# A two-stage transformer kernel on one core: values in high and low parts, up projections with joined products, and three steps moved

## The reference, cut to what matters

```python
def retention_mixer(h_ctx, h_lat, w_in, decay_logit, norm_g, w_out, need_ctx):
    ...
    # per head (4 heads, key width 256, value width 512), for latents and context:
    att = jnp.einsum('bihd,bjhd->bhij', q, k) * decay_mask
    o = jnp.einsum('bhij,bjhv->bihv', att, v)          # "the values"
    ...
def retention_output(o, g, norm_g, w_out):
    ...
    on = ((of - mu) * lax.rsqrt(var + EPS)).astype(g.dtype).reshape(b, n, h * dv) * norm_g
    return (on * jax.nn.silu(g)) @ w_out

# second block, each of two layers:
x = _layer_norm(DEEPNORM_ALPHA * x + h, ln1_g[i], ln1_b[i])
mlp = jnp.einsum('bsf,fd->bsd', jnp.square(jax.nn.relu(jnp.einsum('bsd,df->bsf', x, w_up[i]))), w_down[i])
...
x = _layer_norm(DEEPNORM_ALPHA * x + mlp + ple, ln2_g[i], ln2_b[i])
```

## Time and profile before

| | |
|---|---|
| median of 3 runs | 2045.7 us (2042.88 to 2045.72) |
| the profiled execution | 2045.57 us, span from first to last instruction 2043.8 us |
| PE busy | 2002.7 us, 98% of the span |
| DVE busy | 1289.1 us, 63% |
| ACT busy | 848.2 us, 42% |
| granted clock of PE, mean | 0.995 |
| PE's full-precision values (line 2382) | 41.8 us busy |

### The profile page before, as it was taken

One profiled execution on the slowest core, in us unless ns is written; L12 is line 12 of the kernel. 1 busy time (PEld: TensorE's weight loads), 2 busy tenths in 40 slices (PEclk: granted clock), 3 DMA queues, 4 the chain that ended last, 5 costly groups with the idle time before them and its releaser, 6 DMA issues.

```text
span 2043.8 us, 27094 instructions
## 1 busy us (share of the span) xinstructions
PE 2002.7 (98%) x11112; PEld 1702.3 (83%) x11112; DVE 1289.1 (63%) x1588; ACT 848.2 (42%) x991; POOL 68.4 (3%) x121
## 2 busy tenths in 40 slices
PE   7999999999999999999999999999999999999998
PEld 5778787778888888877779998898899978989997
DVE  3877879556545354586775555766855567677555
ACT  4332323223322122446664443554544346545442
POOL 0000000000111000000000000000000000000000
PEclk9999999999999999999999999999999999999999
DMA  9543444333454343332137655545665554546552
GB/s 342 173 161 124 144 144 139 109 131 107 143 167 157 116 129 129 103 107 100 49 105 217 185 167 163 190 168 167 206 200 191 166 170 157 196 158 214 188 185 81
DMA packets 250734, 319.30 MB, mean 156 GB/s; under 512 B 10097, under 2 KB 166034, under 8 KB 250098
## 3 DMA queue, kind: packets, MB, share of 16 engines
q1 hardware_dynamic: 234880, 262.24, 40.2%
q0 software_dynamic: 14416, 53.14, 7.8%
q10 hardware_dynamic: 1314, 2.18, 0.3%
HBM read 316.47 MB, written 1.05 MB: 155 GB/s over the span
## 4 chain that ended last, share of the span: by engine, by line
PE 82%; DVE 8%; DVEq 4%; ACT 2%; SPq 1%; issue 1%; ACTq 1%; DMA 1%
PE ps L2305 13%; PE ps L2306 13%; PE ps L2300 6%; PE ps L2855 6%; PE ps L2319 5%; PE ps L2315 5%; PE ps L2316 5%; PE ps L2861 5%; PE ps L2865 5%; PE ps L2862 5%; PE ps L2248 4%; PE ps L2772 2%; PE ps L2775 2%; PE ps L2771 2%; DVE w_lo L1239 1%; DVE raw L1370 1%
## 5 line engine op out<-in xcount | busy, mean ns | idle before, releaser
L1239 DVE TENSOR_TENSOR w_lo<-raw,w_hi 128x2048 fp32r<-128x2048 f32 (+1 forms) x244 | 553.3, 2272 | 304.5 <-ACT w_hi L602 303.7
L602 ACT ACTIVATE w_hi<-raw 128x2048 fp32r<-128x2048 f32 (+1 forms) x244 | 461.7, 1897 | 267.3 <-PE ps L2300 157.4
L2305 PE MATMUL ps<-w_hi,big_hi 128*128 128x512 f32 x760 | 299.1, 393 | 0.9 <-DVE big_lo L1729 0.7
L2306 PE MATMUL ps<-w_hi,big_lo 128*128 128x512 f32 x760 | 296.6, 390 | 0.0
L2315 PE MATMUL ps<-hT_hi,w_hi 128*128 128x512 f32 (+1 forms) x512 | 192.5, 381 | 3.1 <-ACT arena L710 2.0
L2316 PE MATMUL ps<-hT_lo,w_hi 128*128 128x512 f32 (+1 forms) x512 | 190.4, 377 | 0.0
L2861 PE MATMUL ps<-h_hi,w_hi 128*128 128x256 f32 x768 | 189.7, 285 | 0.0
L2862 PE MATMUL ps<-h_lo,w_hi 128*128 128x256 f32 x768 | 188.3, 283 | 0.0
L2305 PE MATMUL ps<-w_hi,hT_hi 128*128 128x512 f32 x416 | 168.9, 406 | 4.8 <-DVE hT_lo L1244 4.8
L2305 PEld LDWEIGHTS ps<-w_hi,big_hi 128*128 128x128 f32 x760 | 142.8, 188 | 30.4 <-issue 1.0
L2306 PEld LDWEIGHTS ps<-w_hi,big_lo 128*128 128x128 f32 x760 | 143.0, 188 | 28.8 <-issue 0.5
(11 more groups left out here) (309 smaller groups left out, 3072.5 us busy)
## 6 DMA issues: line engine op xcount, KB each, us to landing
raw<-ffn_w_in SPq DMA_DIRECT2D x88, 512.0 KB, 5.1
raw<-w_in SPq DMA_DIRECT2D x80, 512.0 KB, 4.6
raw<-w_up SPq DMA_DIRECT2D x64, 512.0 KB, 4.7
raw<-w_down SPq DMA_DIRECT2D x64, 512.0 KB, 4.6
raw<-ret_w_in SPq DMA_DIRECT2D x48, 512.0 KB, 5.4
front<-ada_w POOLq DMA_DIRECT2D x24, 1024.0 KB, 5.5
raw<-ffn_w_out SPq DMA_DIRECT2D x40, 512.0 KB, 4.5
raw<-ada_w POOLq DMA_DIRECT2D x64, 256.0 KB, 4.1
```

What stands on the lines that cost most here:

```text
L602: act.activation(SPLIT_HI[PAIR_OF[u]][:, 0:m], raw[:, RAW_OF[u], 0:m], ACT.Copy).then_inc(sem["hi_ready"], 1)
L1239: op(SPLIT_LO[PAIR_OF[u]][:, 0:m], raw[:, RAW_OF[u], 0:m], SPLIT_HI[PAIR_OF[u]][:, 0:m].bitcast(F32), ALU.subtract).then_inc(sem["lo_ready ...
L2305: pe.matmul(out, x[0][:, t * P:(t + 1) * P], w, start=start, stop=False)
L2306: pe.matmul(out, x[1][:, t * P:(t + 1) * P], w, start=False, stop=False)
```

## The change

1. The values of retention heads 0 to 2 are computed as hi*hi, lo*hi and hi*lo. ScalarE writes PT_HI and VN_HI, VectorE PT_LO and VN_LO. VN_LO is written by `values_lo`, on VectorE's list behind the second `weigh()` of the next head; `values` waits for it. The scores are written to another place in the arena, PT_LO over them.
2. The up projection's high products have hi and lo part of x side by side as one moving operand of 512 columns, into two halves of a PSUM bank; a unit has two banks, two units alternate. ScalarE copies the lo half, VectorE adds the hi half, and one more operation does ReLU and square.
3. Rows 2 and 3 of the modulation are copied by VectorE, and both are transposed before head 0's strip goes on; VectorE splits the weights of qb0 between two halves of `rows_split`.
4. Head 0's unit g0 goes to the other banks and doesn't wait for qk_read; the unit g1 does.
5. In layer 1 `ln2_first` stands before `x_lo(0, 6)`, and `ln2_second` before the split of the third unit.

```diff
-        h2_hi = sb("h2_hi", [P, KD, 256], F32R, hT_at)
-        h2_lo = sb("h2_lo", [P, KD, 256], F32R, hT_at + 4 * 2048)
+        h2_both = sb("h2_both", [P, 2, KD, 256], F32R, hT_at)
+        h2_hi, h2_lo = (h2_both[:, j, :, :] for j in range(2))
...
+        def gate_banks(h):
+            return head_banks(h)[0 if h else 1]
...
+        VN_HI = sb("VN_HI", [P, 4, 512], F32R, arena_at + 4 * 4096)[:, :, :]
+        VN_LO = sb("VN_LO", [P, 4, 512], F32R, big_at + 4 * (8192 + 4096))[:, :, :]
+        PT_HI, PT_LO = (sb(name, [P, 6, 256], F32R, arena_at + 4 * a)[:, :, :] for name, a in (("PT_HI", 0), ("PT_LO", 2048)))
...
+        UP_PAIR = (6, 0)
...   ScalarE
             split(FIRST_END["qb0"])
-            front(3)
-            row(0, 8960, 2)
-            front(4)
-            row(1, 9472, 3)
             act.wait_ge(sem["mod_ready"], 4)
...
+                act.wait_ge(sem["sc_read"], h + 1)
+                if h < 3:
+                    act.activation(PT_HI, PT, ACT.Copy).then_inc(sem["pt_hi"], 1)
                 used(f"vb{h}")
-                act.activation(VN[:, :, :], ps[:, a:a + 4, :], ACT.Copy).then_inc(sem["v_read"], 1)
+                act.activation(VN_HI if h < 3 else VN, ps[:, a:a + 4, :], ACT.Copy).then_inc(sem["v_read"], 1)
...
-                    act.activation(HID[:, n % 4, :], bank(UP_BANK[n % 4]), ACT.Relu).then_inc(sem["up_read"], 1)
+                    act.activation(HID[:, n % 4, :].rearrange("p (j n) -> p j n", j=2), ps[:, UP_PAIR[n % 2]:UP_PAIR[n % 2] + 2, 256:512], ACT.Copy).then_inc(sem["up_low"], 1)
...   VectorE
             rows_split(1, 0)
-            split(FIRST_END["qb0"])
+            row(0, 8960, 3)
+            row(1, 9472, 4)
             mod_cols(2, 0, 1)
             mod_cols(3, 0, 3)
             rows_split(0, 4)
+            split(FIRST_END["qb0"])
             rows_split(1, 4)
...
+            def values_lo(h):
+                a = head_banks(h)[0]
+                dve.wait_ge(sem["v_read"], h + 1)
+                lo(VN_LO, ps[:, a:a + 4, :], VN_HI).then_inc(sem["v_lo"], 1)
...
                 weigh()
+                if h:
+                    values_lo(h - 1)
                 ahead(f"qa{h}")
...
                 weigh()
+                if h < 3:
+                    dve.wait_ge(sem["pt_hi"], h + 1)
+                    lo(PT_LO, PT, PT_HI)
                 ahead(f"vb{h}")
...
                 split(base + 1)
+                if l:
+                    ln2_first(base)
                 x_lo(0, 6)
                 split(base + 2)
                 if l == 0:
                     last_residual(1, 1)
                 else:
-                    ln2_first(base)
+                    ln2_second(base, l - 1)
                     split(base + 3)
-                    ln2_second(base, l - 1)
...
-                    dve.wait_ge(sem["up_read"], s.next("up_read"))
-                    op(HID[:, n % 4, :], HID[:, n % 4, :], HID[:, n % 4, :], ALU.mult).then_inc(sem["sq2_ready"], 1)
+                    dve.wait_ge(sem["up_low"], s.next("up_low"))
+                    h = HID[:, n % 4, :].rearrange("p (j n) -> p j n", j=2)
+                    op(h, h, ps[:, UP_PAIR[n % 2]:UP_PAIR[n % 2] + 2, 0:256], ALU.add).then_inc(sem["up_read"], 1)
+                    drain()
+                    stt(out=h, in0=h, scalar=0.0, in1=h, op0=ALU.max, op1=ALU.mult).then_inc(sem["sq2_ready"], 1)
...   TensorE
             to_cols(2, 8960)
+            to_cols(3, 9472)
             pe.wait_ge(sem["h_part"], 4)
             strip(4, "qa0", hT, 0, 4, (0, 1), True, False, (2, 3))
-            to_cols(3, 9472)
...
-                pe.wait_ge(sem["v_read"], h + 1)
-                pe.wait_ge(sem["sc_read"], h + 1)
+                if h < 3:
+                    pe.wait_ge(sem["v_lo"], h + 1)
+                else:
+                    pe.wait_ge(sem["v_read"], h + 1)
+                    pe.wait_ge(sem["sc_read"], h + 1)
...
+                        pe.matmul(bank(a + t), PT_HI[:, m, q], VN_HI[:, j, :], start=(n == 0), stop=False)
+                        pe.matmul(bank(a + t), PT_LO[:, m, q], VN_HI[:, j, :], start=False, stop=False)
+                        i = pe.matmul(bank(a + t), PT_HI[:, m, q], VN_LO[:, j, :], start=False, stop=(n == len(keys) - 1))
...
-                pe.wait_ge(sem["qk_read"], h + 1)
-                feature(a, f"g0{h}", 0, 0)
+                g = gate_banks(h)
+                if h:
+                    pe.wait_ge(sem["qk_read"], h + 1)
+                feature(g, f"g0{h}", 0, 0)
...
-                used(feature(a + 1, f"g0{h}", 1, 0))
+                used(feature(g + 1, f"g0{h}", 1, 0))
+                pe.wait_ge(sem["qk_read"], h + 1)
...
-                    if n >= 4:
-                        pe.wait_ge(sem["up_read"], 16 * l + n - 3)
+                    if n >= 2:
+                        pe.wait_ge(sem["up_read"], 16 * l + n - 1)
                     w = unit(f"U{n}", 0, KD)
                     for j in range(2):
-                        i = chunk(bank(UP_BANK[n % 4])[:, j * 256:(j + 1) * 256], w, j, h2, KD)
+                        out, js = ps[:, UP_PAIR[n % 2] + j, :].rearrange("p (a n) -> p a n", a=2), slice(j * P, (j + 1) * P)
+                        for k in range(KD):
+                            pe.matmul(out, w[0][:, k, js], h2_both[:, :, k, :], start=(k == 0), stop=False)
+                        lows(w)
+                        for k in range(KD):
+                            i = pe.matmul(out[:, 0, :], w[1][:, k, js], h2(k)[0], start=False, stop=(k == KD - 1))
```

More of the change, by code:

```diff
@@ L230, in build @@
                  "xt_full", "xt_read", "xm_ready", "h_part", "front_used", "xc_in", "ada_used", "row_ready", "at_full",
-                 "mod_ready", "qk_read", "g_read", "qkt_full", "qkt_read", "sc_full", "sc_read", "v_read",
+                 "mod_ready", "qk_read", "g_read", "qkt_full", "qkt_read", "sc_full", "sc_read", "v_read", "v_lo", "pt_hi",
                  "rpv_full", "on_ready", "ot_full", "ot_mul", "rg_full", "rg_read", "xa_read", "x0_ready",
@@ L239, in build @@
                  "pv_read", "ba_full", "bb_full", "mix_ready", "mix_hi", "mix_lo", "ple_full", "ple_read", "o_full",
-                 "pg_full", "gl_ready", "gate_ready", "up_read", "sq2_ready", "hid2_hi", "hid2_lo", "dn_full",
+                 "pg_full", "gl_ready", "gate_ready", "up_low", "up_read", "sq2_ready", "hid2_hi", "hid2_lo", "dn_full",
                  "ln_var", "ln_rstd"]
@@ L318, in build @@
         SILU = at(8192, 1024)
-        QK, PT, QKT, ON = at(0, 4, 512), at(0, 6, 256), at(2048, 4, 512), at(2048, 4, 512)
+        QK, PT, QKT, ON = at(0, 4, 512), at(2048, 6, 256), at(2048, 4, 512), at(2048, 4, 512)
         VN, GT, ROPE = at(4096, 4, 512), at(6144, 4, 512), at(9728, 256)
+        VN_HI = sb("VN_HI", [P, 4, 512], F32R, arena_at + 4 * 4096)[:, :, :]
+        VN_LO = sb("VN_LO", [P, 4, 512], F32R, big_at + 4 * (8192 + 4096))[:, :, :]
+        PT_HI, PT_LO = (sb(name, [P, 6, 256], F32R, arena_at + 4 * a)[:, :, :] for name, a in (("PT_HI", 0), ("PT_LO", 2048)))
         G1, G2, T1, T2 = (at(8192 + 384 * n, 384) for n in range(4))
@@ L619, in ahead4 @@
                 act.drain()
-            def row(b, a, n):
-                act.activation(at(a, 512), bank(b), ACT.Copy).then_inc(sem["row_ready"], 1)
             def modulate(d, shift, scale, m, c0, src):
@@ L653, in turned_x @@
                 act.activation((XTC if t >= 2 else XTL)[:, :, (t % 2) * P:(t % 2 + 1) * P], bank((4, 6, 0, 2)[t], 2).rearrange("p (c n) -> p c n", c=KD), ACT.Copy).then_inc(sem["xt_read"], 1)
-            def front(n):
-                act.wait_ge(sem["front_used"], n)
             first_norm(0)
@@ L716, in _ @@
                     act.wait_ge(sem["on_lo"], h)
-                act.activation(GT[:, 0:2, :], ps[:, a:a + 2, :], ACT.Silu).then_inc(sem["g_read"], 1)
+                g = gate_banks(h)
+                act.activation(GT[:, 0:2, :], ps[:, g:g + 2, :], ACT.Silu).then_inc(sem["g_read"], 1)
                 ahead(f"g0{h}")
@@ L2376, in values @@
                 a = head_banks(h)[0]
-                pe.wait_ge(sem["v_read"], h + 1)
-                pe.wait_ge(sem["sc_read"], h + 1)
+                if h < 3:
[3 more added lines that the diff above has]
+                    pe.wait_ge(sem["sc_read"], h + 1)
                 for t in range(4):
                     keys = [(0, 0), (1, 1), (2, 2), (3, 3)] if t < 2 else [(4, 2), (5, 3)]
+                    q = slice((t % 2) * P, (t % 2 + 1) * P)
                     for n, (m, j) in enumerate(keys):
-                        i = pe.matmul(bank(a + t), PT[:, m, (t % 2) * P:(t % 2 + 1) * P], VN[:, j, :], start=(n == 0), stop=(n == len(keys) - 1))
+                        if h == 3:
+                            i = pe.matmul(bank(a + t), PT[:, m, q], VN[:, j, :], start=(n == 0), stop=(n == len(keys) - 1))
+                            continue
+                        pe.matmul(bank(a + t), PT_HI[:, m, q], VN_HI[:, j, :], start=(n == 0), stop=False)
```

(2 more changed lines are left out.)

## The result

The changed kernel takes 2060.7 us (median of 4 runs, 2059.86 to 2061.5), the kernel before, run beside it, 2045.7. The ratio is 1.0077, 95% interval 1.0059 to 1.0094: slower by 0.8%. The profiled execution took 2061.5 us with a span of 2059.7, against 2043.8, so 15.9 us have to be found in the trace.

A forecast was written before the change was run, and what follows sets the result against it. TensorE, busy 98% of the span, was taken as the bound, almost tied with VectorE at head boundaries. Terms +25.8 - 4.6 - 6.7 - 2.4 = +12.1 us on 2045.57 gave 2057.7 us, range 2048.5 to 2065.5.

The forecast's parts named there:

- the boundaries: Three head boundaries: TensorE waits 9.5 us for values_lo; 8.6 us lost at each, +25.8 us in all.
- the front: Front and first gate: earlier row copies and other banks, limited by VectorE's fourth weigh and a clock drop; -4.6 us.
- the up projections: Up projections, 32 units: two column blocks in one instruction cost 0.227 in place of 0.240 us; -6.7 us.
- layer 1's start: Start of layer 1: the 2.25 us wait goes, a 1.7 us wait for w_lo comes, clock stays up; -2.4 us.
- The 36 products: Values of a head: 36 products at 0.227 us take 8.2 us, against 10.3 us before; 2.1 us less.
- 0.5 for qk_read: First gate product at each boundary: ScalarE's query/key copies end after the second strip, so 0.5 us of waiting shows.
- the low part of the scores: Before the values: ScalarE's rounding and VectorE's subtraction of the scores fall before the value strip's end, costed at nothing.
- the clock: Behind each boundary's 9.5 us wait: 3.4 us at half clock, +1.7 us, bounds nothing and twice that.
- (a): Rival: at the boundaries only VectorE's longer chain counts; 2038.8 us, if v_lo comes before 134.4; chance 0.09.
- (b): Rival: waits as forecast, but the clock doesn't fall at the boundaries; 2052.6 us; chance 0.15.
- (c): Rival: the joined instruction saves nothing, or VectorE falls behind in the up stage; 2064.4 us; chance 0.12.
- (d): Rival: no clock loss at 91.8, a weaker one at the boundaries, all but cancelling; 2045.6 to 2050 us; chance 0.06.

The follow-up runs named there:

- early: The changed kernel with values_lo moved directly behind the weight split that ends a head, ahead of both weigh() calls: 2044.9 us, ratio 1.0001 to the kernel before.
- spread_full: The order of `spread` with the values in full precision: 2030.0 us, ratio 0.9928 to the kernel before.
- vals: The kernel before with only the values of heads 0 to 2 in three products: 2074.0 us, ratio 1.0138.
- full: The changed kernel with the values of all heads in full precision, the other four edits kept: 2031.8 us, ratio 0.9937 to the kernel before.
- nogate: `spread` without the other banks for head 0's gate unit g0: 2024.8 us, ratio 0.9903 to the kernel before.
- row: The kernel before with only VectorE's copies of modulation rows 2 and 3 and the moved weight split: 2038.8 us, ratio 0.9968.
- up: The kernel before with only the up projections' joined products: 2038.6 us, ratio 0.9966.
- ln2: The kernel before with only the new order at layer 1's start: 2044.0 us, ratio 0.9993.
- gate: The kernel before with only the other banks for head 0's gate: 2042.2 us, ratio 0.9981.
- spread: `early` with one weigh() moved from the boundary to mid-head and the mask arguments before the other: 2024.3 us, ratio 0.9898 to the kernel before.

## Why the prediction was right, step by step

The forecast was 2057.7 us, the measured time is 2060.7: direction, mechanism and range held, and the size was 3 us short. The steps at the boundaries, at the front and in the up projections are those of the forecast; in the fourth term, layer 1's start, most of the agreement is luck.

*The boundary, +8.6 a head forecast, +9.0, +9.9 and +8.7 measured.* Taken apart at the first boundary: TensorE starts the values 9.55 us later behind its strip (20.43 instead of 10.88 us from the strip's start; forecast 9.5). The 36 products take 2.1 us less than the full-precision ones, less the clock: 135.71 to 145.91 is 10.20 us, 8.2 and 2.0 of half clock (forecast 8.2 and 1.7). The second strip with its wait takes 10.9 instead of 11.9 us (forecast the same). Transposes and first gate product are 2.19 us apart, against 1.72 before; the forecast had 0.5 for qk_read, and the timeline shows it as 0.28 only because its idle time counts from the modelled end. v_lo came where it was put: 137.69 + 2.28 = 139.97 on the old clock, and 4.3 us earlier that is 135.7, the time at which TensorE went on. One step was wrong and cost nothing: the low part of the scores ended 1.0 us behind the value strip (114.56 + 1.75 = 116.31, against 115.28) and not ahead of it.

*The term that was mis-sized is the clock.* I took the 3.4 us at 0.50 behind waits of 4.02 and 2.25 us as what any wait costs: 1.7 us. Behind the wait of 9.4 us the slow stretch was 10.2 us long and began inside the wait, and what was left of it behind the wait depended on when TensorE went on: 2.0, 3.0 and 1.8 us. The sum is 6.8 instead of 5.1, and these 1.7 are nearly all by which the boundaries miss (27.6 to 25.8).

*The front, -4.6 forecast, -4.3 measured.* The steps held: both rows copied by 41.4, a wait of only 0.23 us there, the new wait 2.45 us at 92.22 (forecast 2.6 at 91.8), and a half clock behind it. VectorE's chain started 3.95 us earlier, not 4.4, and `extra()` came 0.4 us later than forecast; that is the 0.3.

*The up projections, -6.7 forecast, -5.6 measured.* The mechanism is right: eight joined products take 1.81 to 1.84 us, 0.226 to 0.230 each, like plain ones of 512 columns. The forecast took 0.240 - 0.227 = 0.013 a pair. In the trace 16 of the old ones take 1.91 us, 0.239 a pair, and eight new ones 1.825 on average, 0.228; that leaves 0.011, and 0.002 x 512 pairs is the 1.1 us that is missing. TensorE doesn't idle ahead of line 3146 (0.0 us on the page), so VectorE's extra addition stayed hidden. The Trainium skill ("TensorE: Matmul & The Clock Gate", section "Wait — 56ns, not 53.3ns?") has a fixed cost of about 2.5 ns for back-to-back products at full clock. This stream, in which each product has a weight load of its own (10636 of each on the page), doesn't bear it out: 1.91 less 1.81 or 1.84 is 0.07 to 0.10 us for eight instructions fewer, 9 to 13 ns each.

*Layer 1's start, -2.4 forecast, -2.2 measured.* The wait for w_lo is 1.62 us (forecast 1.7), and the clock stayed up. But 1.7 of both numbers is a clock loss that the old order showed in the profiled run of the kernel before and in none of the four other runs that keep that order. The order is worth 0.5 us, and that this term came out so near is luck.

*The rivals.* (a) fell: v_lo came at 135.65 where TensorE wanted it near 126.3. Its bound of 134.4 doesn't follow from its own terms: 154.9 less 8.2 and 10.9 is 135.8. With v_lo forecast at 140.0 this decides nothing. `early` shows that its condition could be met, and that its price then was 4.15 and not 2.3 a boundary. (b) and (c) fell by the clock of 0.50 and by the unit's 5.56 us. Of (d) nothing came: the gains were slightly smaller, not larger.

What stays open are the 0.4 us elsewhere, and what decides whether a wait of about 2 us lowers the clock (below).

## What to carry to other kernels

When a product is split into high and low parts, the cost need not be in the arithmetic; it can be in where the extra subtraction stands in the other engine's list. Here 2.28 us of work, put behind 11.7 us that nobody waited for, cost 27.6 us. At the front of the list it still cost 4.15 us at each of the three boundaries, since VectorE's list up to the normalised values was then 2.3 us longer; with one `weigh()` less in that list, a boundary took 2.6 us less than before (85.5 for 88.1). Before a wait is added, read what is queued ahead of its releaser, and look on that engine for the idle slot into which the work that isn't urgent can go; the two moves together turned a loss of 0.8% into a gain of 1.0%, of which 0.6% came from the other edits. Where two engines are tied, shortening one of them shows little until the other is shortened as well: the boundary went from 88.1 to 87.6 us with VectorE's list alone thinned (`spread_full`), and to 85.5 with both. And before a gain of 1 to 2 us is credited to an edit, look where the half-clock stretches lie in both traces: each is worth 1.7 us (3.4 us at half the clock), and they come and go in places that the edit doesn't touch.

## What the runs showed of the hardware

The half clock isn't a fixed price per wait. With 9.4 us of waiting it lasted 10.2 us in six of six boundaries (`vals` and the changed kernel), and began some 6, 4 and 7 us before TensorE's wait ended; with the 5.3 us of `early` it lasted 6.8. Around 2 us the same wait went both ways: 2.45 us at 92.22 in the changed kernel dropped the clock to 0.51, and 2.36 us at the same place in `full` left it at 1.00:

```profile
91.90:95.40 3.50, 3.45 (x20) 3.00 (x20) 3.33 (x2) 0.00 (x0) 0.75 (x1) 1.00 0.46 128
```

and the wait of 2.03 us for the copy of queries and keys, which cost nothing in the kernel before, in `vals` and in `nogate`, was followed by a half clock in `row`, `up` and `ln2`. `row`:

```profile
62.10:65.50 3.40, 3.40 (x9) 2.63 (x8) 3.25 (x6) 1.81 (x2) 0.00 (x0) 0.50 0.91 330
```

The wait of 2.20 to 2.26 us at layer 1's start was followed by 0.50 in the kernel before and by 1.00 in `vals`, `row`, `gate` and `up`. The waits of 1.6 us there left it up, in the changed kernel and in `ln2`. Near 1065 TensorE waits 1.81 us in the kernel before (1064.69), and a half clock follows. No edit touches that place, the wait is 1.81 or 1.82 us in all thirteen profiled runs, and the stretch is there in nine of them and missing in four (`row`, `spread`, `up`, `ln2`). So for a wait of about 2 us the honest forecast is two values, 1.7 us apart.
